# A two-layer trunk on one Trainium2 core: modulation weights used row by row, heads reordered, layer 1's modulation spread over other tiles

## What is computed

```
mod = silu(c) @ ada_w + b            # 6 x 1024: shift, scale, gate, twice
h = rmsnorm(x, g) * (1 + scale1) + shift1
y = mixer(h)                         # layer 0: mLSTM heads and a gated conv; layer 1: stick-breaking attention
x = x + (1 + gate1) * y
h = rmsnorm(x, g') * (1 + scale2) + shift2
x = x + (1 + gate2) * peer_ffn(h)    # 16384 experts, top 16 of each of 8 heads
```

## Time and profile before

| | |
|---|---|
| median of 3 runs | 3645.11 us (3635.3 to 3647.26) |
| profiled execution: its time, its span | 3643.7 us, 3641.7 us |
| busy: PE, DVE, ACT, POOL | 3477.8, 2896.2, 1345.6, 731.3 us |
| mean granted TensorE clock | 0.979 |

### The profile page before, as it was taken

One profiled execution on the slowest core, in us unless ns is written; L12 is line 12 of the kernel. 1 busy time (PEld: TensorE's weight loads), 2 busy tenths in 40 slices (PEclk: granted clock), 3 DMA queues, 4 the chain that ended last, 5 costly groups with the idle time before them and its releaser, 6 DMA issues.

```text
span 3641.7 us, 47773 instructions
## 1 busy us (share of the span) xinstructions
PE 3477.8 (95%) x17076; PEld 3069.8 (84%) x17076; DVE 2896.2 (80%) x4687; ACT 1345.6 (37%) x1926; POOL 731.3 (20%) x443
## 2 busy tenths in 40 slices
PE   2997999999999999999999999999999999999999
PEld 2865899999989888888977567899999999999998
DVE  5585999999966888888764556999999957878884
ACT  2332333444433233222343663334444433333332
POOL 2332444000013221111033003450000022212210
PEclk9997999999999999999999799999999999999999
DMA  4451244565678898988622002344655598989993
GB/s 188 151 173 52 82 141 145 181 224 185 226 261 306 313 326 306 310 309 306 224 87 85 2 12 81 105 157 142 220 193 212 220 337 300 311 291 310 311 302 128
DMA packets 331681, 748.17 MB, mean 205 GB/s; under 512 B 24568, under 2 KB 204792, under 8 KB 329592
## 3 DMA queue, kind: packets, MB, share of 16 engines
q1 hardware_dynamic: 88272, 321.43, 26.2%
q10 hardware_dynamic: 206376, 290.31, 22.3%
q0 software_dynamic: 36864, 134.23, 10.9%
HBM read 626.34 MB, written 119.54 MB: 205 GB/s over the span
## 4 chain that ended last, share of the span: by engine, by line
PE 79%; DVE 10%; DMA 7%; issue 2%; ACT 1%; ACTq 1%; DVEq 0%
PE bank L790 23%; PE bank L791 23%; PE bank L792 23%; DMA ada_w<-ada_dram 6%; PE gbank L982 3%; DVE ada_w L1130 2%; DVE w_lo L1437 2%; DVE gin L1505 1%; DMA gin<-gel_dram 1%; DVE xT L1181 1%; PE gbank L928 1%; PE bank L1070 1%; PE gbank L1070 1%; DVE ada_first L1192 1%; PE gbank L1098 1%
## 5 line engine op out<-in xcount | busy, mean ns | idle before, releaser
L790 PE MATMUL bank<-h_hi,w_hi 128*128 128x448 f32 (+1 forms) x2792 | 1053.2, 377 | 23.4 <-DVE h_lo L1336 18.7
L791 PE MATMUL bank<-h_lo,w_hi 128*128 128x448 f32 (+1 forms) x2792 | 1039.3, 372 | 0.0
L792 PE MATMUL bank<-h_hi,w_lo 128*128 128x448 f32 (+1 forms) x2792 | 1039.2, 372 | 0.0
L427 ACT ACTIVATE w_hi<-raw 128x1024 fp32r<-128x1024 f32 x613 | 648.0, 1057 | 511.0 <-PE bank L792 352.0
L790 PE MATMUL bank<-a_hi,w_hi 128*128 128x448 f32 x2048 | 758.1, 370 | 40.7 <-DVE a_lo L1513 40.7
L791 PE MATMUL bank<-a_lo,w_hi 128*128 128x448 f32 x2048 | 754.6, 368 | 0.0
L792 PE MATMUL bank<-a_hi,w_lo 128*128 128x448 f32 x2048 | 754.3, 368 | 0.0
L381 POOL TENSOR_TENSOR w_lo<-raw,w_hi 128x1024 fp32r<-128x1024 f32 x165 | 436.0, 2643 | 895.8 <-ACT w_hi L427 807.4
L790 PEld LDWEIGHTS bank<-h_hi,w_hi 128*128 128x128 f32 x2792 | 525.4, 188 | 88.6 <-issue 27.4
L792 PEld LDWEIGHTS bank<-h_hi,w_lo 128*128 128x128 f32 x2792 | 524.7, 188 | 61.2
L791 PEld LDWEIGHTS bank<-h_lo,w_hi 128*128 128x128 f32 x2792 | 525.5, 188 | 59.6 <-issue 4.6
(11 more groups left out here) (285 smaller groups left out, 3239.0 us busy)
## 6 DMA issues: line engine op xcount, KB each, us to landing
raw<-stream_dram SPq DMA_DIRECT2D x613, 512.0 KB
gel_dram<-gel ACTq DMA_DIRECT2D x256, 224.0 KB
g_dram<-stage ACTq DMA_DIRECT2D x14, 4096.0 KB, 14.6
gates<-g_dram ACTq DMA_DIRECT2D x128, 448.0 KB
gin<-gel_dram ACTq DMA_DIRECT2D x128, 448.0 KB
ada_w<-ada_dram ACTq DMA_DIRECT2D x80, 512.0 KB
ada_first<-ada_dram ACTq DMA_DIRECT2D x4, 2048.0 KB, 24.5
xT<-x_t_dram ACTq DMA_DIRECT2D x1, 2048.0 KB, 8.7
```

The costliest lines, as they stand in the source:

```text
L427: act.activation(w_hi[:, s, :], raw[:, s, :], ACT.Copy).then_inc(split_hi, 1)
L790: pe.matmul(out, wh, hi(k), start=(k == 0), stop=False)
L791: pe.matmul(out, wh, lo(k), start=False, stop=False)
L792: mm = pe.matmul(out, wl, hi(k), start=False, stop=(k == DC - 1))
```

## The change

The first 16 blocks of `ada` are loaded on SP's queue as eight pieces of 1 MB (shift and scale of one row block), between the first four weight tiles; the seven small loads go to POOL's queue, ahead of its constants. DVE makes the root first and then, for each row block k, its two dots, bias, scale, `hw` and (one block behind) `h_lo`. PE takes the first four input tiles together, row block by row block, six of the eight so and the last two tile by tile. ACT splits the fourth tile early.

Layer 0's other dots begin at input tile 6 for the loads (`ADA_FROM` 11 to 6), and DVE makes ten of them between steps of the gates' row. The convolution moves to tiles 22 to 25, the heads' last product `mix` to tiles 26 to 28, and the first four output tiles are again made together by row blocks, the convolution's four blocks first. Layer 1's 48 dots: two in each of the 8 output tiles of layer 0, one in each V group of layer 0, two in each of the 8 output tiles of layer 1.

```diff
-ADA_FROM = 11
+ADA_FROM = 6
+ADA_OUT = (4 * DC, 8 * DC)
+ADA_V = 6 * DC
@@ SP
-        for s in range(RING):
-            load(0, s)
+        for k in range(DC):
+            if k < RING:
+                load(0, k)
+            sp_.dma_start(ada_first[:, k, :, :], ada[0:2 * DC].rearrange("(s k) p n -> k p s n", s=2)[k]
+                          ).then_inc(S(f"ada_first{k}"), 16)
@@ POOL, ahead of the constants
+        for dst, src in ((adab, ada_b), (gain, gains), (gateb, gate_b), (convw, conv_w), (mnormc, mnorm),
+                         (keysT, keys), (qkn, qk_norm)):
+            pool.dma_start(dst[:], src).then_inc(S("small_landed"), 16)
@@ ACT
-        for t in range(LEAD):
+        for t in range(RING):
             high(t)
@@ ACT, input tiles
-            high(t + LEAD)
+            if m:
+                high(t + LEAD)
-            if m >= HEADS_FROM:
+            if HEADS_FROM <= m < N_IN - 1:
                 head_work(*divmod(m - HEADS_FROM, 4))
+        high(OUT0 + LEAD)
         for k in range(HEADS):
             act.wait_ge(S("conv"), k + 1)
             act.activation(h_hi[:, HEADS + k, :], chT[:, k, :], ACT.Copy).then_inc(S("conv_hi"), 1)
+        for h in range(HEADS - 1):
+            mixed(h)
+        head_work(HEADS - 1, 3)
+        mixed(HEADS - 1)
@@ ACT, projected_out
+                for n in range(2):
+                    ada_load(ADA_OUT[layer] + 2 * m + n)
@@ ACT, v_tiles
-                    if layer == 0 and k in (0, 2, 4):
-                        ada_load(first_ada + k // 2, i * 6 if turn else 0)
+                    if layer == 0 and k == 0:
+                        ada_load(ADA_V + g)
@@ PE
+        def ring_by_rows(t0, ks, by_rows, hi_ready, lo_ready):
+            for n, k in enumerate(ks[:by_rows]):
+                hi_ready(k)
+                for t in range(t0, t0 + RING):
+                    if n == 0:
+                        begin(t)
+                    highs(t, k, n == 0)
+                lo_ready(k)
+                for t in range(t0, t0 + RING):
+                    lows(t, k, False)
+            for t in range(t0, t0 + RING):
+                for k in ks[by_rows:]:
+                    ...
+                    highs(t, k, False)
+                    lows(t, k, k == ks[-1])
-                first_tiles("n0", IN0)
-            elif m >= 2:
+                ring_by_rows(IN0, [*range(DC)], DC - 2, ...)
+            elif m >= RING:
                 h_tile(IN0 + m)
-            if m == 5:
+            if m == 7:
                 pe.wait_ge(S("row_r"), 1)
-        for m in range(N_OUT):
-            h_tile(OUT0 + m, ready=mixed_ready if m == 0 else None)
+        ring_by_rows(OUT0, [*range(HEADS, DC), *range(HEADS)], HEADS, mixed_high, mixed_low)
@@ DVE, start
+        root("n0")
+        for k in range(DC):
+            dve.wait_ge(S(f"ada_first{k}"), 16)
+            for n in range(2):
+                last = dve.tensor_tensor_reduce(ada_first[:, k, n, :], ...)
+            link(last)
+            ...
+            dve.scalar_tensor_tensor(out=hw[:, k, :], ...).then_inc(S("norm_y"), 1)
+            if k:
+                first_low(k - 1)
+        first_low(DC - 1)
@@ DVE, after row_m
+        for n in range(4):
+            first_ada(n)
         dve.wait_ge(S("r_tp"), 1)
         ...
+        for n in range(4, 2 * (11 - ADA_FROM)):
+            first_ada(n)
         dve.wait_ge(S("decay_mm"), 1)
@@ DVE, head_work step 3 of the last head, between hm_var and hm_std
+                if h == HEADS - 1:
+                    ... # conv_lo of the four blocks, mix_low of heads 0 to 2
@@ DVE, input tiles
-            if m >= N_IN - HEADS:
-                convolve(m - N_IN + HEADS)
+            if 22 <= m < 22 + HEADS:
+                convolve(m - 22)
@@ DVE, output(layer)
+                if m < N_OUT - 1:
+                    for n in range(2):
+                        mod_dot(ADA_OUT[layer] + 2 * m + n)
@@ DVE, v_tiles
-                    if layer == 0 and k in (1, 3, 5):
-                        ...
+                    if layer == 0 and k == 1:
+                        mod_dot(ADA_V + g)
```

More of the change, by code:

```diff
@@ L542, in _, with mixed @@
                 row_exps()
-            if m >= HEADS_FROM:
+            if HEADS_FROM <= m < N_IN - 1:
                 head_work(*divmod(m - HEADS_FROM, 4))
+        def mixed(h):
+            act.wait_ge(S("mix"), h + 1)
+            act.activation(h_hi[:, h, :], qT[:, h, :], ACT.Copy).then_inc(S("mix_hi"), 1)
+        high(OUT0 + LEAD)
         for k in range(HEADS):
@@ L813, in norm, with begin, highs, lows @@
             last.then_inc(S("norm_rstd"), 1)
+        def begin(t):
+            pe.wait_ge(split_lo, t + 1)
+            if t >= RING:
+                pe.wait_ge(emptied_sem[EVAC[t - RING]], emptied(EVAC[t - RING], t - RING))
+        def highs(t, k, first):
+            w = slice(k * P, (k + 1) * P)
+            pe.matmul(bank[t % RING][:], w_hi[:, t % RING, w], h_hi[:, k, :], start=first, stop=False)
+            pe.matmul(bank[t % RING][:], w_lo[:, t % RING, w], h_hi[:, k, :], start=False, stop=False)
+        def lows(t, k, last):
+            mm = pe.matmul(bank[t % RING][:], w_hi[:, t % RING, k * P:(k + 1) * P], h_lo[:, k, :], start=False,
+                           stop=last)
+            if last:
+                mm.then_inc(tile_done, 1)
         def first_tiles(tag, t0):
             for t in (t0, t0 + 1):
-                pe.wait_ge(split_lo, t + 1)
-                if t >= RING:
-                    pe.wait_ge(emptied_sem[EVAC[t - RING]], emptied(EVAC[t - RING], t - RING))
+                begin(t)
                 for k in range(DC):
@@ L823, in first_tiles @@
                         pe.wait_ge(S("norm_hi"), normed(tag, "hi") + k + 1)
-                    w = slice(k * P, (k + 1) * P)
-                    pe.matmul(bank[t % RING][:], w_hi[:, t % RING, w], h_hi[:, k, :], start=(k == 0), stop=False)
-                    pe.matmul(bank[t % RING][:], w_lo[:, t % RING, w], h_hi[:, k, :], start=False, stop=False)
+                    highs(t, k, k == 0)
             for t in (t0, t0 + 1):
@@ L908, in _, with mixed_high, mixed_low @@
                 head_work(*divmod(m - HEADS_FROM, 4))
-        def mixed_ready(k):
+        def mixed_high(k):
+            if k < HEADS:
+                pe.wait_ge(S("mix_hi"), k + 1)
+            else:
+                pe.wait_ge(S("conv_hi"), k - HEADS + 1)
+        def mixed_low(k):
             if k < HEADS:
@@ L1294, in head_work @@
                 dve.tensor_scalar(w2, misc[3][:], 1.0 / P, EPS, ALU.mult, ALU.add).then_inc(S("hm_var"), 1)
+                if h == HEADS - 1:
+                    for k in range(HEADS):
+                        dve.wait_ge(S("conv_hi"), k + 1)
+                        dve.tensor_tensor(h_lo[:, HEADS + k, :], chT[:, k, :], h_hi[:, HEADS + k, :].bitcast(F32),
+                                          ALU.subtract).then_inc(S("conv_lo"), 1)
+                    for k in range(HEADS - 1):
+                        mix_low(k)
                 dve.wait_ge(S("hm_std"), h + 1)
@@ L1343, in output @@
                     add_square(f"f{layer}", m - 1)
+                if layer and m == 5:
+                    link(biased(4 * DC, 5 * DC))
+                    columns(3, 1, 3 * DC)
+                if m < N_OUT - 1:
+                    for n in range(2):
+                        mod_dot(ADA_OUT[layer] + 2 * m + n)
             add_square(f"f{layer}", N_OUT - 1)
@@ L1349, in peer @@
             norm(f"f{layer}", 2 * layer + 1)
+            for n in range(2 * N_OUT - 2, 2 * N_OUT):
+                mod_dot(ADA_OUT[layer] + n)
+            if layer:
+                dve.wait_ge(S("ada_used"), 10 * DC)
+                link(biased(5 * DC, 6 * DC))
+                dve.tensor_scalar(g1p[:, 3, :], mod[:, 1, 5 * DC:6 * DC], 1.0, None, ALU.add)
             def step(instructions):
```

121 lines of the change are left out of this document (61 added, 60 removed).

## The result

| | before | after |
|---|---|---|
| median, runs | 3642.88 us (3635.3 to 3647.26), 4 | 3592.27 us (3585.09 to 3596.78), 4 |
| ratio, 95% interval | | 0.9857 [0.984, 0.9873] |
| profiled execution: time, span | 3643.7, 3641.7 us | 3585.1, 3582.9 us |

What follows compares the result with a forecast made beforehand. PE was taken as the bound nearly everywhere. Gains of 11.5 + 10 + 14 − 4 + 60 + 0.5 summed to 92 us, taken from the median 3645.1 to give 3553 us, range 3536 to 3590.

Steps and rivals of the forecast that it cites:

- the heads: Input tiles 11 to 28: the state wait, slow clock after it and a short gap go; gain 10 us, bounds 5 and 11.
- the output tiles: Both layers' output tiles: two dots between x_updates make DVE lag PE; 4 us lost together, bounds 0 and 12 lost.
- the V tiles: Layer 0's V tiles: 32 of 48 dots removed, gaining 60 of the 62.4 us over layer 1; lower bound 41.
- the join: From tile 28's end into the output projection: four tiles end at 29.3 instead of 43.4 us; gain 14, bounds 9 and 17.
- a round at 6.05 us: DVE per output tile: 0.75 + 0.7, 2.4 of dots and 2.2 held back by POOL's split, against PE's 5.44 us.
- rival (c): Output tiles run at the loads' pace, some 6 us a round; just past a 12.3 us round, 3660 us; chance 0.02.
- the last tile catches up: Output tiles: the last has no dots and recovers lag, so 2 us lost per layer was taken instead of 4.
- the wait on `state`: PE's 6.2 us wait for the last head's states, and about 2.5 us of slow clock after it, should go.
- the 62.4 us: Layer 0's V tiles against layer 1's, 688.0 and 625.6 us: explained as 40.7 of waits and some 22 of clock.
- slack spent evenly: V tiles: 21 us of dots and at most 15 of landing fit DVE's 99.0 us of slack, one dot per group.
- rival (a): Layer 0's V tiles gain only in proportion, 41 us, as waits for ada_w stay; total 3572 us, chance 0.12.
- Start: Kernel start to input tile 11: earlier first blocks move tile 11 from 133.6 to 122.1; gain 11.5 us, bounds 0 and 18.

Runs made afterwards that it cites:

- the run without waits: Changed kernel with the one dot of each layer 0 V group made after k = 3, load still at k = 0: 3574.48 us, 0.9813.
- the mixed version: Changed kernel, convolve(3) after tile 26's head step, ACT's input-tile loads last, one dot per layer 0 output tile, eight in odd V groups: 3556.23, repeated 3565.84 us.

## Why the prediction was wrong

Three terms of the sum failed: the heads fell short by 14.9 us (10 forecast, −4.9 measured), the output tiles by 12.9 in layer 0 and some 2 in layer 1, and the V tiles by 11.1. The other differences, 2.6 more at the join and the chance gain of the attention among them, make up part of it, so that 58.8 of 92 us are left.

**Output tiles, the overlap that failed.** I put a round at 6.05 us and the loss at 2 us a layer; it was 14.9 and some 4. Two things were wrong. The sum of 6.05 has no landing in it. The round is a landing of 4.5 to 5.1 us and one dot, of 1.7 to 2.3 on the first buffer, since a load goes out only when the last dot on its buffer is done: 6.98 us. Even my rival (c) had the landing at 3.3 us, read from a load that went out alone (139.83 to 143.14 in the earlier trace rows); loads that went out in pairs took longer in the same trace, 5.3 us from the issue at 144.48 to this dot:

```profile
149.78 1.23 DVE L1130 CUSTOM_DVE_ANT_0 ada_w<-ada_w,cvec 128x1024 f32<-128x1024 f32 x1 [4.17 <-DMA ada_w<-ada_dram]
```

I dismissed that rival by its threshold of 12.3 for a net loss, when the same formula at its own "some 6", or 7, costs 8 to 22 us. And "the last tile catches up" took the eight tiles as evenly spaced; the row-by-row join hands DVE four at once (for which 9.1 us of wait are left even without the landing). Without the landing V starts 11.0 us earlier, without the dots 13.4.

**Heads, the wait that stayed.** I took the wait on `state` as a matter of the last four tiles' load and let it go with the convolution. It kept 5.0, because the moved convolution stands on the same queue in front of an earlier head step; moving one group by one tile gave 9.7. The ACT rounds behind `ada_load` cost tile 10's end the wait I forecast (5; 6.2), and a further 2.6 at tile 13 that I did not. So PE's waits came to 8.8 us where they had been 8.6, and the clock, at 0.95 over 157.9 us in place of 0.98 over 152.9, lost some 8 us in place of 3 (an estimate, (1 − clock) × length). That accounts for the −4.9.

**V tiles.** The mechanism was right, that 16 dots leave almost no `a_lo` wait (2.7, forecast under 8; clock 1.00). The size was not: 48.9 for 60. The missing 11 are no clock and no wait, but the wider distance of the matmuls, a term that the sum doesn't have; in the run without waits it was gone, and what sets it is open. My explanation of the 62.4 as 40.7 of waits and 22 of clock had read the windows' 0.97 only: five stretches of the kernel before between 1368 and 1670, 188 us together, stand at 0.2067, which is 3.6 us, and leave 18 for the clock. The reason I gave, slack spent evenly, was wrong even where the number was near: rival (a)'s lead of one tile is the mechanism, as the 32 dots with one tile of lead (693.7) and with three (642.2) show, and with three tiles even 24 dots cost nothing.

**Start and join** held: 12.0 for 11.5 and 16.6 for 14. The start's number is partly luck, since two parts of it cancel. POOL's issues took about 0.54 us each and not 1.2 (the latency to the first byte set beside that price is another quantity), so ACT's first activation ran at 9.55 and not 13.4:

```profile
4.25 0.54 POOL L367 DMA_DIRECT2D keysT<-keys_dram  x1
...
9.55 0.31 ACT L463 ACTIVATE ones_r<-ones 128x128 fp32r<-128x128 f32 x1 [6.50 <-POOL iota L386]
...
14.46 1.06 ACT L465 ACTIVATE cvec<-cvec 128x1024 f32<-128x1024 f32 x1 [3.30 <-DMA cvec<-c_dram]
...
34.18 1.22 DVE L1266 CUSTOM_DVE_ANT_0 ada_first<-ada_first,cvec 128x1024 f32<-128x1024 f32 x1 [0.89 <-PE gbank L824]
```

But `c` landed later than the 12.5 I took, and POOL's splits stretched the root's two DVE steps to 2.9 and 2.8 us. The first dot came at 34.2 for 34. (`row_m` at 100.5 does not follow from its own numbers either: 112.0 − 10.0 is 102.0. The trace has the first dot behind it at 100.2.) The join's 16.6, though right on PE, didn't reach the end, as the version with whole tiles shows: I summed two stages of which the second, on DVE, swallowed the first.

## What to carry to other kernels

A load issued from a queue that waits for its buffer is as late as the last use of that buffer. Count the round, with a landing time from loads issued as the new ones will be, and give it tiles of lead before giving it fewer dots. Work spread over "slack" costs nothing only if it doesn't itself wait; look at which engine ends the stage after the change before adding the gains of neighbouring stages. And where a stage is longer than its waits and its clock explain, compare the distance of its matmuls along the stage.

## What the runs showed of the hardware

At a granted clock of 1.00 the same matmuls (128 rows by 448 columns) ran at one of two distances, 0.203 or 0.2067 us, and kept one for up to 600 us. Most changes stand at a restart after a wait of 0.4 to 5 us, but not every such wait changes it: the mixed version's first profile has seven of 0.2 to 0.6 us in layer 0 and stayed at 0.203. Nor does every change need one. The repeat of the changed kernel changed at 1224.9 at a single distance of 0.25 us, the version with `convolve(3)` later at 2977.1 at one of 0.30 us, and the version with ACT's loads last at about 1178.6 with no distance over 0.22 us. What decides between the two is open.

512 KB of `ada_w` took 3.3 us from issue to landing among the input tiles of the kernel before, when one load went out alone, and 4.7 us (median) in pairs in the changed kernel's output tiles. In the V tiles the median was 8.5 us in the changed kernel, at a DMA share of 0.86, and up to 12.4 us from issue to dot with two loads per group, at 0.82.

A DVE step beside one of POOL's splits took 3.4 us in place of 1.2, as the dots of the run without loads show.
